# Attention by pairs of heads: scores on two row halves, values as the stationary side, the softmax division moved into the turning product

## The reference

```python
def dsa_attend(q, qi, wi, key_lim, k_all, v_all, ki_all, top_k):
    ...                                   # an indexer picks the top_k admissible keys of each query
    qh = q.reshape(b, nq, A_KV, nh // A_KV, hd)
    logits = jnp.einsum('bqgrd,bqkgd->bqgrk', qh, k_sel).astype(jnp.float32) * hd ** -0.5
    logits = jnp.where(valid[:, :, None, None, :], logits, -jnp.inf)
    p = jax.nn.softmax(logits, axis=-1)
    o = jnp.einsum('bqgrk,bqkgd->bqgrd', p.astype(v_sel.dtype), v_sel)
```

## Time and profile before

| what | us |
|---|---|
| runs, median (lowest to highest) | 1818.67 (1816.83 to 1818.70) |
| profiled execution | 1816.69 |
| its span | 1814.9 |
| attention stage with GLA, from the first `sc` to the first `catT` | 315.2 to 473.9 of the span |
| `catT`, then `y` | 473.9 to 478.1, then to about 543 |
| router, ranking and table of slots | to about 621 |
| 32 experts and one overflow block | to about 1735 |

### The profile page before, as it was taken

One profiled execution on the slowest core, in us unless ns is written; L12 is line 12 of the kernel. 1 busy time (PEld: TensorE's weight loads), 2 busy tenths in 40 slices (PEclk: granted clock), 3 DMA queues, 4 the chain that ended last, 5 costly groups with the idle time before them and its releaser, 6 DMA issues.

```text
span 1814.9 us, 38263 instructions
## 1 busy us (share of the span) xinstructions
PE 1570.0 (87%) x16465; PEld 759.5 (42%) x16465; DVE 618.6 (34%) x1247; ACT 268.5 (15%) x548; POOL 155.6 (9%) x241
## 2 busy tenths in 40 slices
PE   3998888789992299999999999999999999998820
PEld 2664754555652034443443434434434344343310
DVE  1369996433346021121211212212112122121138
ACT  2231116333321000000000000000000000000001
POOL 1024104000111300000000000000000000000031
PEclk7799998655995599999999999999999999999865
DMA  9225549000443799999999999999999999985673
GB/s 347 76 104 189 186 157 346 17 4 3 161 170 115 254 364 402 404 394 407 410 396 409 397 407 409 395 409 409 397 408 394 407 409 396 407 311 214 278 250 109
DMA packets 118001, 531.91 MB, mean 293 GB/s; under 512 B 14338, under 2 KB 32296, under 8 KB 67160
## 3 DMA queue, kind: packets, MB, share of 16 engines
q1 hardware_dynamic: 85556, 471.23, 65.7%
q0 software_dynamic: 12272, 41.26, 7.0%
q10 hardware_dynamic: 20020, 17.10, 2.9%
HBM read 500.18 MB, written 29.37 MB: 292 GB/s over the span
## 4 chain that ended last, share of the span: by engine, by line
PE 74%; DVE 15%; ACT 3%; issue 3%; DMA 3%; POOL 1%; ACTq 1%; SPq 0%; DVEq 0%; POOLq 0%
PE psum L1686 38%; PE psum L1701 19%; DVE raw_ring L906 4%; DVE work L904 4%; PE psum L1649 3%; PE psum L1615 2%; PE psum L1630 2%; PE psum L1677 2%; PE psum L1670 2%; DVE final_work L1273 1%; PE psum L1623 1%; PE psum L1511 1%; POOL slot_dram L1416 1%; DMA raw_ring<-in_b_mod 1%; DMA final_work<-in_g_final 1%
## 5 line engine op out<-in xcount | busy, mean ns | idle before, releaser
L1686 PE MATMUL psum<-weight_ring,expert_work 128*32 128x512 f32 x3888 | 426.5, 593 | 1.8 <-ACT expert_work L817 1.8
L1701 PE MATMUL psum<-weight_ring,expert_work 128*32 128x256 f32 x6336 | 351.2, 381 | 3.5 <-ACT expert_work L821 3.5
L1686 PE MATMUL psum<-raw_ring,expert_work 128*32 128x512 f32 x2448 | 272.2, 598 | 11.8 <-DMA raw_ring<-in_w_gate_up 10.9
L1210 DVE TENSOR_TENSOR expert_work<-psum,expert_work 128x768 f32<-128x768 f32 x33 | 31.6, 957 | 703.5 <-PE psum L1686 703.5
L1701 PEld LDWEIGHTS psum<-weight_ring,expert_work 128*32 128x32 f32 x6336 | 203.2, 110 | 139.4 <-issue 6.4
L1686 PEld LDWEIGHTS psum<-weight_ring,expert_work 128*32 128x32 f32 x3888 | 125.2, 110 | 277.6 <-issue 271.1
L1686 PEld LDWEIGHTS psum<-raw_ring,expert_work 128*32 128x32 f32 x2448 | 77.7, 111 | 183.6 <-issue 166.5
L821 ACT ACTIVATE expert_work<-psum 128x768 f32<-128x768 f32 x33 | 26.7, 810 | 658.4 <-PE psum L1677 646.2
L1511 PE MATMUL psum<-front_ring,work 128*128 128x512 f32 (+2 forms) x320 | 117.5, 528 | 0.0
L1225 DVE TENSOR_TENSOR expert_work<-psum,expert_work 128x768 f32<-128x768 f32 x33 | 31.6, 957 | 192.7 <-PE psum L1701 192.7
L1429 POOL COPY keep<-keep 96x1 int32 (+1 forms) x34 | 6.1, 178 | 982.8 <-PE psum L1670 981.1
(11 more groups left out here) (303 smaller groups left out, 1285.2 us busy)
## 6 DMA issues: line engine op xcount, KB each, us to landing
weight_ring<-in_w_gate_up SPq DMA_DIRECT2D x162, 1024.0 KB, 16.4
weight_ring<-in_w_down SPq DMA_DIRECT2D x132, 1024.0 KB, 16.7
raw_ring<-in_w_gate_up SPq DMA_DIRECT2D x102, 1024.0 KB, 14.8
front_ring<-in_w_mod SPq DMA_DIRECT2D x12, 2048.0 KB
ys_dram<-expert_work ACTq DMA_DIRECT2D x132, 96.0 KB, 8.9
ys_dram<-raw_ring POOLq DMA_DIRECT2D x1, 8448.0 KB, 46.3
front_ring<-in_w_in SPq DMA_DIRECT2D x4, 2048.0 KB
front_ring<-in_w_mod_final SPq DMA_DIRECT2D x4, 2048.0 KB
```

The source lines that it names most:

```text
L1210: local(v.tensor_tensor(eg, gu_ps[:, :, 0:FF4], bg, ALU.add), 0, i)
L1686: last = mm(gu_ps[32 * q:32 * q + 32, b, :].rearrange("p (g n) -> p g n", g=2), lhsT=xT[:, k, 32 * b:32 * b + 32], rhs=w[:, q], start=(k = ...
L1701: last = mm(dn_ps[32 * q:32 * q + 32, b, :], lhsT=x, rhs=w[:, h, q], start=(s_ == 0 and h == 0), stop=(s_ == DNS - 1 and h == 1))
```

## The change

A unit of the prompt is now a pair of heads, r and r + 4, that belong to the two key/value heads (16 units where there were 32). For the pair:

- `sc` makes two products, one on rows 0 to 63 and one on rows 64 to 127, into two PSUM banks. VectorE runs its mask-and-maximum operation twice, one after the other, and negates both maxima in one operation; ScalarE takes two exponentials.
- VectorE has a new piece of work at the step `pT`: it waits for `probs_made`, takes the reciprocal of both row sums, and scales the identity with each into two diagonal 128x128 matrices (`diag`, semaphore `diag_ready`). TensorE's `pT` waits for `diag_ready` instead of `probs_made`, and the turn is a full product with the diagonal matrix as the moving side instead of a transpose.
- `pv` has the values (64 columns) stationary and the turned probabilities moving, so the result comes out turned: head r in partitions 0 to 63, head r + 4 in 64 to 127. VectorE only copies it, to `catAT`.
- `catT` turns the GLA result alone (4 transposes a tile instead of 8), and `y` reads `catAT` for its first four blocks. `w_out` comes in an order of rows to match, in three DMAs where there was one.
- The six blocks for `raw_ring` are issued after the last `y` instead of the last `catT`.

The core of the diff:

```diff
-UNITS = [(SAMPLE, 0), (SAMPLE, 1)] + [(t, h) for t in range(4) for h in range(NH)]
+PAIRS = NH // 2
+UNITS = [(SAMPLE, 0), (SAMPLE, 1)] + [(t, r) for t in range(4) for r in range(PAIRS)]
...
             for t in range(T):
-                filled(sp, JOB[("catT", t)])
+                filled(sp, JOB[("y", t)])
             sp.wait_ge(rows_in, ROW_DMAS * 16)
             for k in range(6):
                 gu_weights(0, 0, k)
-            for t in range(T):
-                filled(sp, JOB[("y", t)])
...
+                    for gr in range(2):
+                        c = 2 * (u % 3) + gr
+                        order(v.tensor_tensor_reduce(out=prob[u % 3][:, gr * n:(gr + 1) * n], in0=bank(j, gr)[:, 0:n],
+                                                     in1=score[t][:, 0:n], scale=HD ** -0.5, scalar=NEG,
+                                                     op0=ALU.add, op1=ALU.max, accum_out=amx[:, c:c + 1]))
                     note(dve, done)
+                    c = 2 * (u % 3)
+                    v.tensor_scalar(negm[:, c:c + 2], amx[:, c:c + 2], -1.0, None, ALU.mult).then_inc(logits_max, 1)
+                elif kind == "pT":
+                    u = UNIT[s[1:]]
+                    m, c = 1 if t == SAMPLE else 2, 2 * (u % 4)
+                    dve.wait_ge(probs_made, u + 1)
...
+                    order(v.reciprocal(rinv[:, c:c + m], ars[:, c:c + m]))
+                    for gr in range(m):
+                        ins = v.tensor_scalar(diag[u % 2][:, gr * P:(gr + 1) * P], ident, rinv[:, c + gr:c + gr + 1], None, ALU.mult)
+                    ins.then_inc(diag_ready, 1)
                 elif kind == "pv":
...
+                        v.tensor_copy(catAT[:, s[2], tok], bank(j)[:, 0:P]).then_inc(done, 1)
...
+                    if t != SAMPLE:
+                        for gr in range(2):
+                            ps = slice(HD * gr, HD * gr + HD)
+                            last = mm(bank(j, gr)[:, 0:NKEYS[t]], lhsT=qaT[ps, h, tok], rhs=kaT[ps, 0:NKEYS[t]], start=True, stop=True)
...
                 elif kind in ("pT", "pTnew"):
                     u = UNIT[s[1:]]
-                    pe.wait_ge(probs_made, u + 1)
+                    pe.wait_ge(diag_ready, u + 1)
...
-                        last = tr(group(j)[:, x * P:(x + 1) * P], prob[u % 3][:, x * P:(x + 1) * P], ident)
+                    for gr in range((1 if t == SAMPLE else 2) if kind == "pT" else 0):
+                        for x in range(n // P):
+                            at_ = gr * n + x * P
+                            last = mm(group(j)[:, at_:at_ + P], lhsT=prob[u % 3][:, at_:at_ + P], rhs=diag[u % 2][:, gr * P:(gr + 1) * P],
+                                      start=True, stop=True)
                 elif kind == "pv":
...
                     for x in range(nb):
-                        last = mm(bank(j)[:, 0:P], lhsT=turned_p[:, x * P:(x + 1) * P], rhs=val[:, x, :],
-                                  start=(x == 0), stop=(x == nb - 1 and t != SAMPLE))
+                        for gr in ((s[2],) if t == SAMPLE else range(2)):
+                            ps = slice(HD * gr, HD * gr + HD)
+                            at_ = x * P if t == SAMPLE else (gr * nb + x) * P
+                            last = mm(bank(j)[ps, 0:P], lhsT=(Vs if t == SAMPLE else va)[:, x, ps], rhs=pTs[u % 2][0][:, at_:at_ + P],
+                                      start=(x == 0), stop=(x == nb - 1 and t != SAMPLE))
...
-                    for k in range(KD):
-                        src = catA[0:R, t, k * P:(k + 1) * P] if k < 4 else rg[0:R, t, (k - 4) * P:(k - 3) * P]
-                        last = tr(group(j)[:, k * R:(k + 1) * R], src, ident[0:R, 0:R])
+                    for k in range(4):
+                        last = tr(bank(j)[:, k * R:(k + 1) * R], rg[0:R, t, k * P:(k + 1) * P], ident[0:R, 0:R])
```

More of the change, by code:

```diff
@@ L287, in build @@
         qaTs = csg
-        osum = [cc[:, 0:64], cc[:, 64:128]]
-        pT = [at.take(512), at.take(512)]
+        diag = [at.take(2 * P) for _ in range(2)]
         amx = at.take(16)
@@ L460, in build @@
                 last_step[("out", 0)] = last_step[("out", 1)] = s
-        parts = [2 if c[0] in ("mod", "kv") else 1 for c in chunks]
+        parts = [{"mod": 2, "kv": 2, "out": 3}.get(c[0], 1) for c in chunks]
         need = []
@@ L494, in chunk_cols @@
             if kind == "out":
-                return [(0, CW, w_out[:, :, n * CW:(n + 1) * CW])]
+                return []
             at_ = {"qa": QA, "qkg": QG, "vg": VG, "rg": RG}[kind]
@@ L1083, in _ @@
[L1083 to L1087 removed]
+                    if t == SAMPLE:
+                        c = 2 * (u % 3) + (kind == "scnew")
+                        mx = amx[:, c:c + 1]
+                        order(v.tensor_tensor_reduce(out=prob[u % 3][:, n0:n0 + n], in0=group(j)[:, 0:n],
+                                                     in1=score[t][:, n0:n0 + n], scale=HD ** -0.5, scalar=NEG,
+                                                     op0=ALU.add, op1=ALU.max, accum_out=mx))
+                        note(dve, done)
+                        m0 = amx[:, 2 * (u % 3):2 * (u % 3) + 1]
+                        if kind == "scnew":
+                            order(v.tensor_tensor(m0, m0, mx, ALU.max))
+                            v.tensor_scalar(negm[:, 2 * (u % 3):2 * (u % 3) + 1], m0, -1.0, None, ALU.mult).then_inc(logits_max, 1)
+                        continue
@@ L1617, in _ @@
                 elif kind in ("pT", "pTnew"):
                     u = UNIT[s[1:]]
-                    pe.wait_ge(probs_made, u + 1)
+                    pe.wait_ge(diag_ready, u + 1)
+                    n = min(NKEYS[t], PAST)
                     if kind == "pTnew":
-                        last = tr(bank(j)[0:DEC, 0:P], prob[u % 3][:, PAST:PAST + DEC], ident)
-                    for x in range(min(NKEYS[t], PAST) // P if kind == "pT" else 0):
-                        last = tr(group(j)[:, x * P:(x + 1) * P], prob[u % 3][:, x * P:(x + 1) * P], ident)
+                        last = mm(bank(j)[0:DEC, 0:P], lhsT=prob[u % 3][:, PAST:PAST + DEC], rhs=diag[u % 2][:, 0:P], start=True, stop=True)
@@ L1646, in _ @@
                         if t == SAMPLE:
-                            last = sample_product(j, n, catT, w)
+                            last = sample_product(j, n, lambda k: (catAT if k < 4 else catT)[:, k, SEQ:NTOK], w)
                         for k in range(KD if t != SAMPLE else 0):
-                            last = mm(bank(j, n)[0:R, :], lhsT=catT[:, k, tok], rhs=w[:, k, :], start=(k == 0), stop=(k == KD - 1))
+                            last = mm(bank(j, n)[0:R, :], lhsT=(catAT if k < 4 else catT)[:, k, tok], rhs=w[:, k, :], start=(k == 0), stop=(k == KD - 1))
                 elif kind == "hT":
```

80 lines of the change are left out of this document (34 added, 46 removed).

## The result

The changed kernel takes 1827.05 us (median of seven runs, 1818.15 to 1830.18) against 1818.71 for the kernel before (seven runs, 1816.83 to 1821.77): ratio 1.0038, 95% interval 1.0021 to 1.0054. It is slower, by 7 us by the ratio and 8 by the medians, where 13.5 on top of the profiled execution, 1832 in all, had been forecast. The profiled execution is 1827.16 us, its span 1825.4, 10.5 more than before.

A forecast was written before the change was run, and what follows sets the result against it. The attention stage was taken as bound by TensorE, mostly at half clock. Terms 14 + 3 + 3.6 + 1 - 2.1 - 6.9 + 0.9 = 13.5 on 1816.69 gave 1830, stated as 1832 for the runs' median; range 1814 to 1850.

The forecast's parts named there:

- The wait: TensorE stands ahead of each pair's turn until VectorE has reduced and made the diagonals: 1.90 to 2.70 us, 16 times.
- The four waits behind a `go`: After each go TensorE stops at the next turn for VectorE's work: 3 to 5 us at each of five, +3 net.
- The last two turns: Tail of the attention: the last two turns have no scores beside them, +1 us.
- The fifth go: One of five go steps counted inside the attention stage, each stopping TensorE for 3 to 5 us.
- 2.1 us of gain at `catT`: At `catT`, 20 transposes instead of 40: -2.1 us.
- The halves: Score products on two row halves and value products on two column halves run side by side, 2n passes each per pair.
- rival C: In the attention, halves don't run side by side; scores and values cost double, 160 passes more: 1857 us, chance 0.08.
- the 8n passes of a pair: Scores, turn and values of a pair with n key blocks take 8n passes instead of 10n; 1.7 us saved in tile 3.
- The clock: In the attention, two pairs with n = 3 and three with n = 4 run at 1.00: net -6.9 us.
- rival B: TensorE's clock stays high through most of the attention: about 1808 us, chance 0.14.
- D: TensorE's clock never rises in the attention and y starts low: about 1848 us, chance 0.12.
- 3 for the sample's passes: The sample's turn takes sixteen passes instead of eight transposes, twice, with a little VectorE time ahead: +3.6 us.

The follow-up runs named there:

- the early diagonals: Changed kernel with VectorE making the diagonals of pair u-1 behind the reductions of pair u, one iteration earlier: 1778.19 us, ratio 0.9790 to the kernel before.
- the values first: Kernel with the early diagonals, the values' step put ahead of the GLA step in each iteration: 1774.17 us with products, 1773.52 with transposes.

## Why the prediction was right, and where not

**The wait** was read right, in place and in size. For 512, 384, 256 and 128 keys the sum said 2.70, 2.43, 2.17 and 1.90 us; measured are 2.58, 2.31, 2.05 (once 2.39) and 1.81. In tile 3 the two reductions with their gaps took 1.58 us instead of 1.72 and the two scalings 0.48 instead of 0.56, while 0.15 us from the scaling's end to the turn were not in the sum. The four waits behind a `go`, one of them in the sample's second unit, are 6.2 to 7.3 us, in which the pair's own wait is included; the forecast had 3 to 5 on top of it. The last two turns have no reduction ahead of them and wait 1.07 us each. The sum had a whole 2.70 for each of them and 1 us more for both, 4.3 us too many; the sample's first turn waited 1.54 where it had about 0.2.

**The fifth go** was put in the wrong place. With 16 pairs instead of 32 heads the list has fewer iterations for the same GLA steps, and the last `go` now falls behind the last turn. Its VectorE work holds the copies of the values, and `catT` waits 3.7 us for one of these banks (the second line of the waits above). The forecast had counted a fifth wait inside the stage and 2.1 us of gain at `catT`; `catT` lost 3.0. Waits of stage and `catT` together: 20.8 us before, 59.6 after, 38.8 more; the sum had 36.8 + 1 + 3, about 41.

**The halves** run side by side. The four passes of a pair's scores, of 64 rows and 256 columns, took 1.23 us at 0.50 (the rows of tile 1 above), and in tile 3 they took 1.13 at 1.00, as the two of one head did before (1.12 at the same clock). So rival C falls, and the 8n passes of a pair stand. The price of a pass at 0.50, 0.2133 us, fits too: value steps of eight and of six passes took 1.91 and 1.48 us before.

**The clock** has two sides. Where the pairs run high came out as chosen: two turns of tile 2 and three of tile 3 ran at 1.00, and one of tile 3 took 3.74 us at 0.50. The forecast had taken this number between two bounds and not worked it out, so that it came out is luck; one turn of tile 1 ran at 1.00 as well. Rivals B and D each hold for a part of the stage: 63 us of it are at 1.00 where there were 31, by windows cut at the clock's steps. Not in the sum was that GLA steps in these stretches gain as well: the last three took 0.65, 0.63 and 1.06 us, against 1.12, 1.07 and 1.91 at 0.50 before, and those beside tile 2's turns likewise, some 4 us in all. With it TensorE's busy time in stage and `catT` fell by 31.3 us, where the terms of the sum come to 29 (14 less the 36.8 of waits in it, 3 for the sample's passes, -2.1 and -6.9).

**The reason that was given against rival B was wrong.** The forecast set aside the rule that transposes don't lift the clock, on the ground that the clock rose right behind a stretch that held eight of them. One stretch with transposes and other products in it can't say what the transposes did there. Pairs of kernels can that differ in this (the last two also in what VectorE scales): mean clock 0.57 with transposes and 0.69 with products in the changed kernel, 0.60 and 0.72 in the kernel before, 0.70 and 0.85 with the early diagonals, 0.74 and 0.78 with the values first. The Trainium skill, "TensorE: Matmul & The Clock Gate", in its part on PE-mode transpose, says that full clock isn't engaged in that mode. The runs agree in direction, in all four pairs. Where transposes are mixed with products the sentence is too strong: the last heads of the kernel before ran at 1.00, and four transposes of one of them took 0.66 us there, 1.11 at 0.50:

```profile
462.91 0.66 PE L1623 MATMUL psum<-keep,work 128*128 128x128 f32 x4
```

By that the forecast's reading that the clock rises behind unbroken PE work was too simple. It doesn't fit its own rows either: ahead of 343.5 TensorE was busy for 4.41 of 5.00 us, and the 17.9 unbroken us at 0.50, with transposes in every head, brought no rise. Across kernels, the one with 64 columns was busy for 88% of its stage at 0.54, the one with the early diagonals for 83% at 0.85. What made the clock rise at 459.6, in heads of the same make as those ahead of them, no run shows.

**Stalls against clock:** the forecast held that the stalls speak for the low level. With them gone the clock was higher, from 0.69 to 0.76 and 0.85 (0.71, 0.79 and 0.84 from the first turn on), with the work hardly changed (72.5, 73.0 and 74.7 at full speed). That is one profiled execution each; the times, 1827, 1793 and 1778, go with it. So fewer stalls went with a higher clock; but the kernel before stood at 0.50 from 441.7 to 459.6 without a stall.

**The rest:** `y` lost 0.6 us of the 0.9 allowed for a low start. The loads cost nothing: the ten blocks had moved by about 580, 29 us after their issue where 31 were forecast, and the queue's next work is at 591.56. The last 2.8 us, behind the routing, were not in the sum and lie within what the same stretch varies from one execution to another; the kernel's own runs spread over 12 us.

Against 13.5 forecast stand 10.5 in the profiled span: 5 us too many in stage and `catT`, 2 too few behind. The mechanism, VectorE's order of work as the price of the change, was right, and the experiments above show it. That the total came within 3 us owes something to errors that cancel: the last two turns and the GLA steps at 1.00 were priced some 8 us too high, the `go` behind the last turn, the sample's waits and the stretches behind `y` too low.

## What to carry to other kernels

When an engine gets a new small piece of work on which a fast engine waits, look at what stands ahead of it in its own list; here 0.7 us of work (a reciprocal and two scalings) had TensorE wait 1.8 to 2.6 us in eleven of sixteen pairs and 6.2 to 7.2 us in three, and making it an iteration earlier turned a loss of 0.4% into a gain of 2.1%. Where TensorE's clock moves between its levels, passes saved need not be time saved: hold a kernel with the edit against one without it and read the granted clock beside the busy time. Read more than one execution, and the stretch ahead of the edit as well: one profiled execution here was 4.7 us ahead of another before it came to anything in which the two kernels differ. And when a loop gets shorter, see what else was spread over its iterations.

## What the runs showed of the hardware

- Replacing transposes by products of twice the passes made the kernel before no slower (0.9981, 0.9965 to 0.9996), at a mean clock of the stage of 0.72 for 0.60, and over the whole span of 0.902 to 0.912 in ten runs for 0.892 to 0.900 in thirteen.
- Moving 64 columns for 128 in the values' products saved 0.1 of 1.91 us in a step whose eight weight loads took 1.83, and the kernel was 0.7% slower, at a mean clock of 0.54 for 0.60.
- Products on two column halves, in alternation, took 0.068 us each at 1.00 (sixteen in 1.09 us), and 0.099 one half after the other.
